# A delta rule whose values are computed ahead, a scan whose sums are added in halves of 64 rows, and norms that end by token tiles

## The reference

```python
# gated delta rule, per chunk of tokens
v_new = u - w @ state
o = qd @ state + qkc @ v_new
state = gl[..., None, None] * state + jnp.swapaxes(kd, -1, -2) @ v_new

# SSD scan, per direction; 4 chunks of 128 tokens, 32 heads
a_cum = jnp.cumsum(a, axis=-1)
seg = a_cum[..., :, None] - a_cum[..., None, :]
decay = jnp.exp(jnp.where(lower, seg, -jnp.inf))
y_diag = jnp.einsum('bcqgn,bcsgn,bgrcqs,bcsgrp->bcqgrp', cm, bm, decay, xs)

# the norms
y = xf * lax.rsqrt(jnp.mean(xf * xf, axis=-1, keepdims=True) + NORM_EPS)
(tf - mu) * lax.rsqrt(var + NORM_EPS_2) * g + b
```

## Time and profile before

| what | value |
| --- | --- |
| median of three runs | 4400.04 us |
| the profiled execution | 4395.62 us |
| its span in the trace | 4393.8 us |
| TensorE busy (PE) | 4041.8 us, 92% |
| TensorE weight loads (PEld), beside PE | 3316.7 us, 75% |
| VectorE busy (DVE) | 2572.2 us, 59% |
| ScalarE busy (ACT) | 1633.3 us, 37% |
| GpSimd busy (POOL) | 107.4 us, 2% |
| mean granted TensorE clock | 0.95 |

### The profile page before, as it was taken

One profiled execution on the slowest core, in us unless ns is written; L12 is line 12 of the kernel. 1 busy time (PEld: TensorE's weight loads), 2 busy tenths in 40 slices (PEclk: granted clock), 3 DMA queues, 4 the chain that ended last, 5 costly groups with the idle time before them and its releaser, 6 DMA issues.

```text
span 4393.8 us, 51780 instructions
## 1 busy us (share of the span) xinstructions
PE 4041.8 (92%) x20660; PEld 3316.7 (75%) x20660; DVE 2572.2 (59%) x4060; ACT 1633.3 (37%) x2876; POOL 107.4 (2%) x199
## 2 busy tenths in 40 slices
PE   5869989898789899999999999999899999999988
PEld 5759768777669778887888678767788787777776
DVE  6667365544666332456567743776566667545865
ACT  3343232134343232333444243553334343334532
POOL 0000000000000000000000000000000000000000
PEclk9979799999889799989999999999899999999999
DMA  6502146632202223323221222133232312231233
GB/s 221 154 10 87 44 133 191 192 108 87 68 20 82 67 87 91 99 96 112 82 92 58 87 88 90 56 123 118 80 116 80 105 58 84 82 91 58 84 103 120
DMA packets 216641, 417.93 MB, mean 95 GB/s; under 512 B 16384, under 2 KB 61472, under 8 KB 214608
## 3 DMA queue, kind: packets, MB, share of 16 engines
q1 hardware_dynamic: 197584, 335.12, 24.5%
q0 software_dynamic: 18816, 79.49, 5.2%
HBM read 378.89 MB, written 35.67 MB: 94 GB/s over the span
## 4 chain that ended last, share of the span: by engine, by line
PE 76%; DVE 14%; ACT 6%; issue 2%; DMA 2%; SPq 0%; DVEq 0%; ACTq 0%; POOL 0%; POOLq 0%
PE ps L595 56%; PE ps L104 13%; DVE arena L121 4%; ACT arena L192 3%; PE ps L110 3%; DVE arena L136 3%; PE ps L2179 2%; DVE spl L121 2%; DVE X L121 1%; ACT sph L192 1%; DVE HF L121 1%; DVE sm L142 1%; PE ps L2175 1%; DVE arena L130 0%; ACT HTh L192 0%
## 5 line engine op out<-in xcount | busy, mean ns | idle before, releaser
L121 DVE TENSOR_TENSOR spl<-ring,sph 128x1024 fp32r<-128x1024 f32 (+2 forms) x556 | 651.5, 1179 | 800.9 <-ACT sph L192 799.3
L192 ACT ACTIVATE sph<-ring 128x1024 fp32r<-128x1024 f32 (+2 forms) x556 | 562.2, 1021 | 873.0 <-PE ps L595 667.6
L595 PE MATMUL ps<-sph,HTh 128*128 128x512 f32 (+3 forms) x1728 | 685.1, 396 | 9.7 <-ACT sm L192 5.5
L595 PE MATMUL ps<-spl,HTh 128*128 128x512 f32 (+3 forms) x1728 | 639.5, 370 | 0.0
L595 PE MATMUL ps<-sph,HTl 128*128 128x512 f32 (+3 forms) x1728 | 637.9, 369 | 0.0
L192 ACT ACTIVATE arena<-ps 128x512 f32<-128x512 f32 (+2 forms) x574 | 316.5, 564 | 720.9 <-PE ps L595 478.2
L595 PE MATMUL ps<-HTh,sph 128*128 128x512 f32 x1376 | 548.1, 398 | 22.3 <-DVE spl L121 16.0
L595 PE MATMUL ps<-HTh,spl 128*128 128x512 f32 x1376 | 539.3, 392 | 0.0
L595 PE MATMUL ps<-HTl,sph 128*128 128x512 f32 x1376 | 539.2, 392 | 0.0
L104 PE MATMUL ps<-arena 64*128 64x128 f32 (+8 forms) x2328 | 393.0, 351 | 60.5 <-ACT arena L192 33.4
L595 PE MATMUL ps<-sph 128*128 128x512 f32 x992 | 406.3, 410 | 9.7 <-DVE spl L121 9.7
(11 more groups left out here) (197 smaller groups left out, 5212.5 us busy)
## 6 DMA issues: line engine op xcount, KB each, us to landing
ring<-in_w_in SPq DMA_DIRECT2D x264, 512.0 KB, 3.7
ring<-in_ada_w SPq DMA_DIRECT2D x80, 512.0 KB, 4.2
ring<-in_w_down SPq DMA_DIRECT2D x44, 512.0 KB, 3.3
ring<-in_w_gate SPq DMA_DIRECT2D x40, 512.0 KB, 4.0
ring<-in_w_up SPq DMA_DIRECT2D x40, 512.0 KB, 4.6
ring<-in_w_mem SPq DMA_DIRECT2D x32, 512.0 KB, 3.4
ring<-in_w_out SPq DMA_DIRECT2D x32, 512.0 KB, 3.8
ring<-in_w_br_ssd SPq DMA_DIRECT2D x32, 512.0 KB, 3.8
```

Of the source, the lines that this page charges most:

```text
L121: self.e.tensor_tensor(o, a, b, op).then_inc(*self.done.up())
L192: self.e.activation(o, a, f, **kw).then_inc(*self.done.up())
L595: ins = pe.e.matmul(o, l, r, start=k0 == 0 and i == 0 and not b.pairs, stop=k0 + b.ks == b.kt and i == 3 * b.ks - 1 and (c0 > 0 or not b.p ...
```

## The change

The delta rule: the own-token part of the values of tile m + 1 is issued (`values_pe`) right after the state part of tile m, before TensorE waits for VectorE's copy. The bank is opened by a one-row zeroing matmul, and the products are only added (`add`). `SG` is in two buffers, so VectorE's update waits for `sg` alone; its copy to `VN` now waits for the output of the step before. The banks of the three results are fixed.

The scan: the running sums are computed once per layer transposed (`CUMT`, one row per head and direction, rows 0 to 63 for one direction and 64 to 127 for the other). `segments_pe` takes both banks of an n at once, and the adding matmuls have a column of the identity, 64 rows high, broadcast as weights and the sums as moving data, the two directions in turn.

The norms: the root takes scale and epsilon itself, tile by tile, and the last tile is scaled in two halves by two engines. The chunks ahead of the first projection are split straight out of PSUM. The layer norm's epsilon goes into the root as well, and its last tile is scaled in halves.

```diff
@@ -106,6 +106,11 @@
+    def add(self, o, l, r, stop=False):
+        self.e.matmul(o, l, r, start=False, stop=stop).then_inc(*self.done.up())
+        self.t += 0.21
+        return self.now()
...
@@ -340,7 +349,8 @@
-                     inv=(3, 4, 5), state=(2, 3, 4, 5), inv_early=(3, 0, 1), state_early=(2, 3, 0, 1))
+                     inv=(3, 4, 5), state=(2, 3, 4, 5), inv_early=(3, 0, 1), state_early=(2, 3, 0, 1), vn=(2, 3),
+                     og=(4,), sg=(5,), cfin=(2, 5), og_early=(0,), sg_early=(1,), cfin_early=(2, 1))
...
@@ -772,12 +785,22 @@
+                at[key, "xn", "half"] = q.now()
...
-            norm_squares(a, key, marks)
-            rstd_act(a, key, sm[:, 600:604])
-            norm_scale(a, key)
+            j = ar(ARENA - 1024, 1024)
+            a.wait_ge(at["eps"])
+            for m in range(4):
+                ss = sm[:, 600 + m:601 + m]
+                a.wait_ge(at[marks[m]])
+                a.act(j, X[:, m, :], ACT.Square, acc=ss)
+                at[key, "root", m] = a.act(ss, ss, ACT.Sqrt, scale=1.0 / D, bias=eps[:, 0:1])
+            a.wait_ge(at[key, "rstd", 0])
+            at[key, "xn", 1] = a.act(xn[:, 1, :], X[:, 1, :], ACT.Copy, scale=sm[:, 601:602], par=True)
+            a.wait_ge(at[key, "rstd", 3])
+            at[key, "xn", 3] = a.act(xn[:, 3, 512:1024], X[:, 3, 512:1024], ACT.Copy, scale=sm[:, 603:604], par=True)
...
@@ -791,10 +814,13 @@
-            v.wait_ge(at[key, "square", 3])
-            rstd_dve(v, key, sm[:, 600:604], 1.0 / D, 1e-6)
+            v.wait_ge(at[key, "root", 2])
+            at[key, "rstd", 0] = v.rec(sm[:, 600:603], sm[:, 600:603])
...
+            v.wait_ge(at[key, "root", 3])
+            at[key, "rstd", 3] = v.rec(sm[:, 603:604], sm[:, 603:604], par=True)
+            at[key, "xn", "half"] = v.ts(xn[:, 3, 0:512], X[:, 3, 0:512], sm[:, 603:604], None, ALU.mult)
...
@@ -828,16 +854,17 @@
-                if k % 2 == 0:
+                if scale is None:
+                    f = bank_of[key, "ht", k][:, :]
+                elif k % 2 == 0:
...
-                    if scale is None:
-                        t = v.cp(f, bank[:, :], par=k > 1)
-                    else:
-                        t = v.ts(f, bank[:, :], scale[:, k:k + 1], bias[:, k:k + 1], ALU.mult, ALU.add, par=k > 1)
+                    t = v.ts(f, bank[:, :], scale[:, k:k + 1], bias[:, k:k + 1], ALU.mult, ALU.add, par=k > 1)
...
+                if scale is None:
+                    at["free", (key, "ht", k)] = at[key, "htl", k]
...
@@ -1522,21 +1549,22 @@
             yield (0.3, 1.2)
+            values_pe(pe, l, 0)
             for m in range(5):
                 if m < 4:
-                    b, b2, b3 = [take(pe, (n, l, m), pool("state")) for n in ("vn", "og", "sg")]
-                    pe.wait_ge(at["nw", l], at["qt", l])
+                    SG = SGs[m % 2]
                     pe.wait_ge(at["sgo", l, m])
...
                         pr, ti = (h % 2) * 64, h // 2
-                        hs = slice(64 * h, 64 * h + 64)
                         if h == 1:
                             pe.own()
-                        at["vn_t", l, m] = pe.mm(b[:, hs], [
-                            (TT[:, m, h * 128:h * 128 + 128], TOK[:, m, 512 + 64 * h:576 + 64 * h]),
-                            (NW[pr:pr + 64, m, ti * 128:ti * 128 + 128], SG[pr:pr + 64, ti, :])])
+                        at["vn_t", l, m] = pe.add(bank_of["vn", l, m][:, 64 * h:64 * h + 64], NW[pr:pr + 64, m, ti * 128:ti * 128 + 128],
+                                                  SG[pr:pr + 64, ti, :], stop=h == 3)
+                    if m < 3:
+                        values_pe(pe, l, m + 1)
                 yield (0.5, 0)
                 if m < 4:
+                    b2, b3 = [take(pe, (n, l, m), pool(n)) for n in ("og", "sg")]
                     pe.wait_ge(at["vn", l, m])
...
@@ -1552,8 +1580,16 @@
-                    finish_pe(pe, l, "c", m - 2, OCc)
+                    finish_pe(pe, l, "c", m - 2, OCc, pool("cfin"))
...
+        def values_pe(pe, l, m):
+            bank = take(pe, ("vn", l, m), "vn")
+            pe.wait_ge(at["nw", l], at["qt", l])
+            pe.e.matmul(bank[:, 0:256], NFr[0][0:1, :], zero.to_broadcast([1, 256]), start=True, stop=False)
+            for h in range(4):
+                pe.add(bank[:, 64 * h:64 * h + 64], TT[:, m, h * 128:h * 128 + 128], TOK[:, m, 512 + 64 * h:576 + 64 * h])
...
@@ -1752,19 +1788,19 @@
-            at["sgo", l, 0] = v.zero(SG)
+            at["sgo", l, 0] = v.zero(SGs[0])
...
-                    v.wait_ge(at["vn_t", l, m])
+                    v.wait_ge(at["vn_t", l, m], at["og", l, m - 1] if m else None)
...
-                    v.wait_ge(at["sg_t", l, m], at["og", l, m])
+                    v.wait_ge(at["sg_t", l, m])
...
-                        t = v.stt(SG[:, ti, :], SG[:, ti, :], eL2[:, m, ti:ti + 1], bank_of["sg", l, m][:, ti * 64:ti * 64 + 64],
+                        t = v.stt(SGs[(m + 1) % 2][:, ti, :], SGs[m % 2][:, ti, :], eL2[:, m, ti:ti + 1], bank_of["sg", l, m][:, ti * 64:ti * 64 + 64],
...
@@ -1961,6 +1997,7 @@
+        CUMT = ar(R4 + 2688, 256)
...
@@ -2153,12 +2190,17 @@
-            yield (2.5, 2.4)
+            bank = take(pe, ("cumt", l), "seg")
+            for m in range(4):
+                for d, tri in enumerate((U, Lr)):
+                    r = 64 * d + 32 * (m // 2)
+                    at["cumt_t", l] = pe.mm(bank[r:r + 32, m % 2 * 128:m % 2 * 128 + 128], [(AA[:, m, 32 * d:32 * d + 32], tri)])
+            yield (2.9, 2.4)
...
-                for d, tri in enumerate((U, Lr)):
+                for d in range(2):
...
@@ -2167,23 +2209,29 @@
                             at["yd", l, n - 2] = pe.mm(by[:, c0:c0 + 64], [(ES[n % 2][:, 0, h, :], XS[:, pg, pm, c0:c0 + 64])])
-                    if n < 32:
-                        g, m, q = SSD[n]
-                        h0 = 32 * d + 8 * g + 4 * q
-                        bank = take(pe, ("seg", l, n, d), "seg")
-                        pe.wait_ge(at["aa", l], at["nfr"])
-                        pe.e.matmul(bank.rearrange("p (h t) -> p h t", h=4), NFr[0][:, :], bc(NFr[1 + d][:, :], 1, 4),
-                                    start=True, stop=False)
-                        pe.t += 0.23
-                        for h in range(4):
-                            ins = pe.e.matmul(bank[:, h * 128:(h + 1) * 128],
-                                              AA[:, m, h0 + h:h0 + h + 1].to_broadcast([128, 128]), tri, start=False, stop=h == 3)
-                            pe.t += 0.22
-                        ins.then_inc(*pe.done.up())
-                        at["seg", l, n, d] = pe.now()
+                    if n < 32 and d == 0:
+                        segments_pe(pe, l, n)
                     if d == 1 and n in (4, 12, 20):
...
                     yield (1.5, 1.5)
+        def segments_pe(pe, l, n):
+            g, m, q = SSD[n]
+            pair = [take(pe, ("seg", l, n, d), "seg") for d in range(2)]
+            pe.wait_ge(at["cumt", l], at["nfr"])
+            for d in range(2):
+                pe.e.matmul(pair[d].rearrange("p (h t) -> p h t", h=4), NFr[0][:, :], bc(NFr[1 + d][:, :], 1, 4),
+                            start=True, stop=False)
+            for h in range(4):
+                for d in range(2):
+                    rows, one = slice(64 * d, 64 * d + 64), 64 * d + 32 * (m // 2) + 8 * g + 4 * q + h
+                    ins = pe.e.matmul(pair[d][:, h * 128:(h + 1) * 128], ident[rows, one:one + 1].to_broadcast([64, 128]),
+                                      CUMT[rows, m % 2 * 128:m % 2 * 128 + 128], start=False, stop=h == 3)
+                    if h == 3:
+                        ins.then_inc(*pe.done.up())
+                        at["seg", l, n, d] = pe.now()
+            pe.t += 1.2
 
...
@@ -2242,6 +2290,8 @@
+            v.wait_ge(at["cumt_t", l])
+            at["cumt", l] = at["free", ("cumt", l)] = v.cp(CUMT, bank_of["cumt", l][:, 0:256], par=True)
...
@@ -2760,10 +2810,14 @@
+                if m == 3:
+                    x = X[:, m, 0:512]
+                    at["xnorm", l, "half"] = v.ts(x, x, MVr[:, m, 1:2], NMR[:, m:m + 1], ALU.mult, ALU.add)
...
-                at["xnorm", l, m] = a.act(X[:, m, :], X[:, m, :], ACT.Identity, scale=MVr[:, m, 1:2], bias=NMR[:, m:m + 1])
+                x = X[:, m, 512 if m == 3 else 0:1024]
+                at["xnorm", l, m] = a.act(x, x, ACT.Identity, scale=MVr[:, m, 1:2], bias=NMR[:, m:m + 1])
...
@@ -2773,14 +2827,14 @@
-                        at["var", l, m] = v.ts(MVr[:, m, 1:2], MVr[:, m, 1:2], 1e-5, None, ALU.add)
+                        at["var", l, m] = v.now()
...
-                    at["sd", l, m] = a.act(MVr[:, m, 1:2], MVr[:, m, 1:2], ACT.Sqrt)
+                    at["sd", l, m] = a.act(MVr[:, m, 1:2], MVr[:, m, 1:2], ACT.Sqrt, bias=eps[:, 1:2])
```

More of the change, by code:

```diff
@@ L160, in zero, with fill @@
         return self.now()
+    def fill(self, o, x):
+        self.e.memset(o, x).then_inc(*self.done.up())
```

(7 more changed lines are left out.)

23 lines of the change are left out of this document (12 added, 11 removed).

## The result

The changed kernel takes 4344.28 us (median of four runs, 4337.58 to 4351.44) where the kernel before, in the same comparison, takes 4397.43. The ratio is 0.9881, 95% interval 0.9859 to 0.9903, so 52 us faster (43 to 62). The forecast was 4362, 38 us faster, with a range of 4337 to 4382. The profiled execution took 4351.44 us with a span of 4349.7, 44 us less than the 4393.8 before; it was the slowest of the four.

A forecast was written before the change was run, and what follows sets the result against it. TensorE was taken as the bound, 76% of the chain of waits. Scan 30, state passes 5 and seams 7, less 3 waiting, make 39, 38 kept: 4395.62 to 4357.6, plus 4.4 for the median, 4362 us; range 4337 to 4382.

The forecast's parts named there:

- The scan, 30 less 3 of waiting: Scan, both layers: paired 64-row passes save 33 us, less 3.2 for transposed sums, leaving 30; 3 us of waiting taken off.
- Rival 1: Scan: the 64-row halves run fully beside each other, 57 us instead of 30, time 4337 by the median; chance 0.12.
- rival 4: Scan: alternating halves does nothing on this pattern, so the scan costs 3 us more, 4391 by the median; chance 0.06.
- The transposed sum: Scan, new in each layer: 16 passes at about 0.10, 1.6 us each, 3.2 in both layers.
- Rival 2: Scan: ScalarE bounds the pairs; one in two waits 0.5 us, 16 us in place of 3, time 4375; chance 0.18.
- nothing moves across main slots: Scan: claimed that nothing on TensorE or ScalarE moves across main slots; no size of its own.
- the forecast's 3.5 us: Scan: TensorE's work between two pairs, two main slots and four products, covering ScalarE's 2.28 us with one other job.
- The state passes, 5: Delta rule's state passes: grouped products and filled gaps save 2.5 us per layer, 5 us in two layers.
- The forecast's split: State passes, per layer: 0.3 us net a step for four steps from fewer changes of form, 1.04 from two filled gaps.
- rival 3: State passes return to full clock, giving back some 17 us per layer; 4345 for one layer, 4328 for two; chance 0.10.
- The seams, 7: Seams between blocks: three norm seams 3.0, first projection 1.9, layer norm 1.6, kernel's end 0.4; between 3 and 10 us.
- Rival 5: Scan: the clock falls from 0.99 towards 0.59, making the kernel slower, 4437 if it holds for 150 us; chance 0.04.

## Why the prediction was right, and where its sizes were off

**The scan, 30 less 3 of waiting.** The pairs came out as worked out: 1.84 us for the 1.83 of the forecast, 33 us over the 64 pairs, and full rows or missing turns give back 32 and 31 of it. Rival 1 is out (1.09 and not 0.80), and rival 4 with it. Two terms around the pairs were mis-sized. The transposed sum costs 0.58 us per layer, not 1.6, so 1.2 instead of 3.2. And instead of 3 us of waiting for ScalarE, TensorE's idle time in the two scan windows fell, by 1.8 and 2.2 us. 33 - 1.2 + 4.0 = 36, where the windows of the whole change have 35.0 and those of the scan alone 40, and both some 38 at an equal clock. Rival 2 is out with the idle time of 0.0 before the masks. What of the idle time fell is the wait before the products with the exponentials, 5.3 to 3.0. The sentence that nothing moves across main slots was wrong: five pairs of a layer moved behind main matmul 7440, and pairs have at least the two main slots between them that the forecast gave them, in half of the cases more. That leaves ScalarE more time than the forecast's 3.5 us, and may be why its 3 us of waiting didn't come; no run separates this from the grouping.

**The state passes, 5.** Alone they give 7.5 (2.6 to 12.7). The gap was filled and the changes of form went as said, and the stretches of the first profile are 3.8 and 3.6 us shorter (110.97 to 107.17, 110.76 to 107.21), of which 0.6 to 0.8 is the seam in them, as the run of the seams alone has it (110.19 and 110.15). The forecast's split isn't borne out: with the values not ahead the stretch is as short (106.63), so in the one trace that there is, the filled gaps show as idle time that went (1.0) and not as time saved. What the forecast kept apart as rival 3, a clock that comes back, happens partly and in some executions: where it does, the stretch is 3 to 7 us shorter still, and no execution of these kernels came near the 17 us per layer of that rival. By its number alone rival 3 would look right, since its 4345 for one layer is the 4344.28 that was measured; by the traces it is chance, as most of what goes beyond the forecast is the scan's. In the first profile both stretches are of the long group (107.2, against a mean of 104.9). That is part of why this profile shows 44 us where the medians give 52; another 3.1 us of it lie ahead of main matmul 1212, which starts at 492.06 before and 495.15 after, and at 488.35 in the other execution of the changed kernel. What decides between the groups in a given execution stays open. That the clock of this stretch can be brought back by dense work put between its small products is shown by the four added matmuls.

**The seams, 7.** Alone they give 9.2 (5.3 to 13.2), near the forecast, but by other terms. The three norm seams were to give 3.0 and give some 1.0: TensorE's idle time falls by 0.75 and 0.44 in two, and doesn't fall in the third. The forecast let each root come while the next square runs at no cost. But both are ScalarE's, one after the other, and the third seam hangs on ScalarE from the first square on, so that roots and table load between its squares (1.57 apart for 1.24) took back all that the tail gave. The layer norm's idle time falls by 1.17 and not 1.6, and the end gives nothing that is seen. The first projection gives more than its 1.9: from main matmul 5950 to 6400 the changed kernel is 3.7 us shorter (118.5 to 114.8), 2.4 of it idle time and the rest the clock, with 20 us at 1.2 GHz instead of 24. The clock varies here too: the ten traces with this part of the change have 112.2 to 116.1 us, the four without it 118.5 to 119.2, and the 116.1 has the same 24 us at 1.2 GHz as those. So the waits were sized about right, and what goes beyond them is the clock.

**Rival 5.** The clock in the scan windows is 0.99 as before, so this rival is out.

**The range.** Its upper end was given as rival 2 with a third more of its waiting. A third of 16 us is 5, which gives 4380 and not 4382; nothing hangs on it.

So the sign, the mechanism and the price of the largest term were right. The 14 us between 38 and 52 (43 to 62, so they are 5 to 24) are, by these windows, a transposed sum that costs less (2), waiting that didn't come with idle time that went (7), and the clock in the state passes (some 5: the mean stretch is 5.8 us shorter per layer, 0.7 of it the seam, where 2.5 was forecast). That the seams' total came out near 7 is luck in part, as norms sized too high met a clock that wasn't in the forecast.

## What to carry to other kernels

In this kernel 64-row products paid only where neighbours sat on different halves. Keep the two streams in turns and count an entry and an exit for each group (0.09 and 0.10 us here), which argues for few and long groups. Where a stretch of small products shows a granted clock far below 1, time the stretch over several executions before judging an edit in it, and try a few dense matmuls that do nothing: four of 0.23 us per step gave back more than they cost, twelve just what they cost. Before an instruction is split into four and spread over an engine's program, look whether that engine waits there; where it doesn't, as in the third norm seam, the pieces count in full. To compare two traces, subtract the starts of the same main matmul, and end the window where the side work of both is done.

## What the runs showed of the hardware

- Sixteen passes with 32-column weights that write different quarters of the partitions took 0.58 us, 0.036 each, against 0.068 for halves in turns and 0.107 for full rows (1.71 / 16). No run tells how much of it is the smaller weights and how much that neighbours write different quarters.
- Cutting the contracted rows from 64 to 32 changed nothing (1.09 for sixteen passes in both), nor did 64 instead of 128 without turns by much (1.64 against 1.71).
- The granted clock of the same program in the same stretch differed between executions: the changed kernel had 58.0 and 58.0 us at 1.2 GHz in one (107.17 and 107.21 us long) and 51.2 and 44.4 in the other (103.85 and 102.88).
- Dense matmuls whose result is thrown away raised the clock of the stretch from 0.73 to 0.88 and 0.90. Three times as many raised it to 0.86 and 0.87.
- In the third norm seam ScalarE loaded a table, 1.28 us, ahead of the first root, both where that root stood behind all four squares and where it stood behind the first.
